# GpSimd folds three modulation vectors, scores run two heads ahead, and a query chunk moves in between the heads of two memory attentions

## What is computed

```
q = (h @ w_q).reshape(bsz, seq, MEM_HEADS, MEM_HEAD_DIM)
k, v = jnp.split(mem_n @ w_kv, 2, axis=-1)
s = jnp.einsum("bshd,bmhd->bhsm", q, k).astype(jnp.float32) * (MEM_HEAD_DIM ** -0.5)
p = jax.nn.softmax(s, axis=-1).astype(v.dtype)
o = jnp.einsum("bhsm,bmhd->bshd", p, v).reshape(bsz, seq, D_MODEL)
return o @ w_o
```

```
mod = jax.nn.silu(c) @ w_mod[l] + b_mod[l]
sh1, sc1, gt1, sh2, sc2, gt2 = jnp.split(mod[:, None, :], N_MOD, axis=-1)
```

## Time and profile before

| | |
|---|---|
| timed runs | 1748.21, 1750.21, 1751.40 us; median 1750.21 |
| span of the profiled execution | 1743.7 us; what lies around a span is seen only in the timed runs |
| busy share of the span | PE 88%, PEld 76%, DVE 50%, ACT 38%, POOL 9% |
| A, B, C: scores to output projection | 178 to 200, 506 to 550, 608 to 630 us |

### The profile page before, as it was taken

One profiled execution on the slowest core, in us unless ns is written; L12 is line 12 of the kernel. 1 busy time (PEld: TensorE's weight loads), 2 busy tenths in 40 slices (PEclk: granted clock), 3 DMA queues, 4 the chain that ended last, 5 costly groups with the idle time before them and its releaser, 6 DMA issues.

```text
span 1743.7 us, 35055 instructions
## 1 busy us (share of the span) xinstructions
PE 1536.5 (88%) x14790; PEld 1321.3 (76%) x14790; DVE 875.3 (50%) x1263; ACT 659.4 (38%) x869; POOL 149.6 (9%) x188
## 2 busy tenths in 40 slices
PE   9999999999999999999999999799998564656568
PEld 8999899988989989998899799698874232323234
DVE  5765466645665556664587688956641010101011
ACT  5445355435444435543566744525441000000001
POOL 5800000000000000000106011130010000000000
PEclk9999999999999999999999999999999678787879
DMA  7765566774744757664454343002899999999995
GB/s 251 242 218 176 188 168 193 225 258 149 262 143 155 249 181 205 192 194 165 134 161 155 97 152 117 26 27 76 314 391 410 431 432 431 430 429 430 431 431 250
DMA packets 238133, 417.16 MB, mean 239 GB/s; under 512 B 13698, under 2 KB 213929, under 8 KB 228009
## 3 DMA queue, kind: packets, MB, share of 16 engines
q1 hardware_dynamic: 237817, 414.59, 66.0%
q10 hardware_dynamic: 176, 0.53, 0.1%
HBM read 414.04 MB, written 1.05 MB: 238 GB/s over the span
## 4 chain that ended last, share of the span: by engine, by line
issue 47%; PE 42%; DVE 4%; POOL 4%; ACT 3%; DMA 1%; DVEq 0%; SPq 0%; POOLq 0%; ACTq 0%
PE bank L429 4%; PE bank L431 4%; PE bank L430 4%; PE bank L1919 2%; PE bank L445 2%; PE bank L447 2%; PE bank L446 2%; PE bank L1075 1%; PE bank L1077 1%; PE bank L457 1%; PE bank L761 1%; PE bank L1076 1%; PE bank L458 1%; PE bank L459 1%; DVE cy L1433 1%
## 5 line engine op out<-in xcount | busy, mean ns | idle before, releaser
L250 DVE TENSOR_TENSOR w_lo<-w_raw,w_hi 128x2048 fp32r<-128x2048 f32 (+2 forms) x178 | 400.3, 2252 | 249.9 <-ACT w_hi L243 246.3
L243 ACT ACTIVATE w_hi<-w_raw 128x2048 fp32r<-128x2048 f32 (+2 forms) x178 | 334.0, 1881 | 152.4 <-DMA w_raw<-in_ffn_w_down_dram 61.7
L429 PE MATMUL bank<-h_hi,w_hi 128*128 128x256 f32 x1168 | 325.3, 279 | 7.0 <-DVE h_lo L639 3.7
L430 PE MATMUL bank<-h_lo,w_hi 128*128 128x256 f32 x1168 | 324.4, 278 | 0.0
L431 PE MATMUL bank<-h_hi,w_lo 128*128 128x256 f32 x1168 | 324.4, 278 | 0.0
L429 PEld LDWEIGHTS bank<-h_hi,w_hi 128*128 128x128 f32 x1168 | 220.3, 189 | 8.4 <-issue 8.3
L2799 PE MATMUL bank<-w_exp_four,xeT 128*32 128x256 f32 x1600 | 133.3, 502 | 99.0 <-DMA w_exp_four<-in_w_up_dram 59.2
L430 PEld LDWEIGHTS bank<-h_lo,w_hi 128*128 128x128 f32 x1168 | 220.4, 189 | 0.0
L431 PEld LDWEIGHTS bank<-h_hi,w_lo 128*128 128x128 f32 x1168 | 220.3, 189 | 0.0
L2799 PEld LDWEIGHTS bank<-w_exp_four,xeT 128*32 128x32 f32 x1600 | 67.0, 142 | 164.4 <-issue 87.5
L2932 ACT ACTIVATE sg<-bank 128x256 f32<-128x256 f32 x16 | 6.1, 384 | 391.4 <-PE bank L2799 391.4
(11 more groups left out here) (537 smaller groups left out, 3130.9 us busy)
## 6 DMA issues: line engine op xcount, KB each, us to landing
w_exp_four<-in_w_up_dram SPq DMA_DIRECT2D x13, 4096.0 KB, 33.3
w_exp_four<-in_w_down_dram SPq DMA_DIRECT2D x13, 4096.0 KB, 33.6
w_exp_four<-in_w_gate_dram SPq DMA_DIRECT2D x12, 4096.0 KB, 33.3
w_raw<-in_ffn_w_gu_dram SPq DMA_DIRECT2D x88, 512.0 KB, 5.1
w_raw<-in_w_in_dram SPq DMA_DIRECT2D x54, 512.0 KB, 4.6
w_mod<-in_w_mod_dram SPq DMA_DIRECT2D x24, 1024.0 KB, 6.9
w_raw<-in_ffn_w_down_dram SPq DMA_DIRECT2D x44, 512.0 KB, 4.2
w_raw<-in_mem_w_kv_dram SPq DMA_DIRECT2D x32, 512.0 KB, 4.6
```

The source lines that it names most:

```text
L243: e.activation(whi[slot][:, 0:w], raw[slot][:, 0:w], ACT.Copy).then_inc(S["hi_ready"], 1)
L250: e.tensor_tensor(wlo[slot][:, 0:w], raw[slot][:, 0:w], whi[slot][:, 0:w].bitcast(F32), ALU.subtract).then_inc(S["lo_ready"], 1)
L429: e.matmul(dst, whi[slot][:, lo:hi_], bh[:, k, :], start=begin, stop=False)
L430: e.matmul(dst, whi[slot][:, lo:hi_], bl[:, k, :], start=False, stop=False)
```

## The change

Three things. The vectors 1, 0 and 4 are folded on GpSimd (`fold`): each side buffer is multiplied by its part of silu(c), the buffers are added up, and the two halves of the sum too, so that 1024 columns are left; four matmuls with a column of ones (`modulate_folded`) then sum over the partitions, at the last head. Those attentions run `by_parts`: scores and softmax of two heads ahead of the first turn, then scores of head h+2 behind the turn of head h. In the memory attentions the query gemm has three chunks, and the fourth is a `chunk_in_parts` whose halves lie behind the first scores and in head 0; the scores wait for their own query chunk alone. All other attentions go as before.

```diff
-        gemm(4, cols(A["mem_w_q"][l]), fm_chunk(*into), act_chunk=copy_fm(qT), ready=[tx], act_ready=[tx],
+        gemm(3, cols(A["mem_w_q"][l]), fm_chunk(*into), act_chunk=copy_fm(qT), ready=[tx], act_ready=[tx],
              beside={j: mod_load(4, 2 + j) for j in range(2)} if l else None)
+        fold(vector)
+        q_evacs = st.evac_a
+        keys_ready, values_ready = (S["act_evac"], q_evacs - 3), dve_evacs()
+        last_queries = chunk_in_parts(cols(A["mem_w_q"][l], first=768), [fm_part(*into, f) for f in range(2)],
...
-        to = attention(4, 2, 256 ** -0.5, score, vv, (pb0, pb1), ptb, [act_evacs(), dve_evacs()], free=[all_used()],
-                       vector=vector)
+        to = attention(4, 2, 256 ** -0.5, score, vv, (pb0, pb1), ptb,
+                       lambda h: [values_ready, (S["act_evac"], q_evacs - 2 + h)], free=[all_used()],
+                       vector=vector, parts=last_queries)
...
+    fold(0)
     k_first = keys2_part(0)
...
-                   causal=causal, free=[all_used()], vector=0, beside={h: lambda: next(memory_side) for h in range(8)})
+                   causal=causal, free=[all_used()], vector=0, parts=memory_side)
...
+        def by_parts():
+            tp = {h: softmax(h, scores(h)) for h in range(2)}
+            next(parts, None)
+            for h in range(heads):
+                tc = turn(h, tp[h])
+                if h + 2 < heads:
+                    tp[h + 2] = softmax(h + 2, scores(h + 2))
+                next(parts, None)
+                if h == heads - 1:
+                    modulate_folded(vector)
+                tl = values(h, tc)
+                tls.extend([tl] * kts)
+            return tl
...
+    def fold(v_):
+
+        n_ = MOD_ORDER.index(v_)
+        scaled = {}
+        for j in range(4):
+            scaled[j] = pool.do(lambda e, j=j: e.tensor_tensor(
+                side[j][:, :, :], side[j][:, :, :], csil[:, 2 * j:2 * j + 2].rearrange("p (k a) -> p k a", a=1).broadcast_to((P, 2, D)),
+                ALU.mult), (side_in[j], 16 * (n_ + 1)), t_cw)
+            if j % 2:
+                t = pool.do(lambda e, j=j: e.tensor_tensor(side[j - 1][:, :, :], side[j - 1][:, :, :], side[j][:, :, :], ALU.add),
+                            scaled[j - 1], scaled[j])
+                scaled[j - 1] = t
+        t = pool.do(lambda e: e.tensor_tensor(side[0][:, :, :], side[0][:, :, :], side[2][:, :, :], ALU.add), scaled[0], scaled[2])
+        t = pool.do(lambda e: e.tensor_tensor(side[0][:, 0, :], side[0][:, 0, :], side[0][:, 1, :], ALU.add), t)
+        folded[v_] = t
...
+            for c in range(4):
+                ins = e.matmul(G[3][32 * c:32 * c + 32, 0:MW], cw[:, :, :].rearrange("p k n -> p (k n)")[:, 64 - v_:96 - v_],
+                               side[0][:, 0, c * MW:(c + 1) * MW], start=True, stop=True)
+            ins.then_inc(mod_used, 4)
```

More of the change, by code:

```diff
@@ L684, in norm_to_features, with attention @@
         return split_features(turn_rows(xn, rows), gain, free)
-    def attention(heads, kts, scale, score, v, pbuf, ptbuf, ready, causal=None, free=(), vector=None, beside=None, behind=None, ahead=None):
+    def attention(heads, kts, scale, score, v, pbuf, ptbuf, ready, vector=None, causal=None, free=(), parts=None, beside=None, behind=None, ahead=None):
         t_soft, t_pt, t_pv = {}, {}, {}
@@ L696, in scores @@
             b = h % 2
-            w = list(ready) + ([xfree[b]] if xfree[b] else []) + ([t_soft[h - 2]] if h >= 2 else [])
+            w = list(ready(h) if callable(ready) else ready) + ([xfree[b]] if xfree[b] else []) + ([t_soft[h - 2]] if h >= 2 else [])
             tok = None
@@ L774, in attention, with by_heads @@
         tls = []
[L775 to L796, removed]
+        def by_parts():
[11 more added lines that the diff above has]
+            return tl
+        def by_heads():
+            ts = scores(0)
+            tp = softmax(0, ts)
+            for h in range(heads):
+                if h + 1 < heads:
+                    ts = scores(h + 1)
+                if h == 0 and "first" in beside:
+                    beside["first"]()
+                if h in ahead:
+                    ahead[h]()
+                tc = turn(h, tp)
+                if h + 1 < heads:
+                    tp = softmax(h + 1, ts)
+                if h in beside:
+                    beside[h]()
+                tl = values(h, tc)
+                tls.extend([tl] * kts)
+                if h in behind:
+                    behind[h]()
+            return tl
+        tl = by_parts() if parts else by_heads()
         tiles_of[tl] = tls
@@ L830, in build @@
     t_cw0 = pool.do(lambda e: e.memset(cw[:, :, :], 0.0))
+    t_cw0 = pool.do(lambda e: e.memset(cw[:, 1, 0:1], 1.0), t_cw0)
     t_z0 = pool.do(lambda e: e.memset(zT[:, :, 0:CONV1 - 1], 0.0))
@@ L861, in modulate, with modulated, modulate_folded, run_pe @@
         if j == 3:
[L862 to L869, removed]
+            modulated(n_)
+    def modulated(n_):
+        done = (mod_used, 4 * n_ + 4)
+        if n_ == 0:
+            t = dve.do(lambda e: e.tensor_copy(mrow[:, :], G[3][:, 0:MW]), done)
+        else:
+            t = dve.do(lambda e: e.tensor_tensor(mrow[:, :], mrow[:, :], G[3][:, 0:MW], ALU.add), done, t_mod["row"])
+        bank_free[3] = [t]
+        t_mod["row"] = t
+    t_mod, folded = {}, {}
+    def fold(v_):
[12 more added lines that the diff above has]
+        folded[v_] = t
+    def modulate_folded(v_):
+        n_ = MOD_ORDER.index(v_)
+        free = list(bank_free[3])
+        def run_pe(e):
+            for w in free:
+                e.wait_ge(*w)
+            e.wait_ge(*folded[v_])
+            for c in range(4):
+                ins = e.matmul(G[3][32 * c:32 * c + 32, 0:MW], cw[:, :, :].rearrange("p k n -> p (k n)")[:, 64 - v_:96 - v_],
+                               side[0][:, 0, c * MW:(c + 1) * MW], start=True, stop=True)
+            ins.then_inc(mod_used, 4)
+        pe.raw(run_pe)
+        modulated(n_)
     mem_in = nc.alloc_semaphore("mem_in")
@@ L989, in mem_attention @@
             gemm(1, cols(W, first=D + 768), tm_chunk(*features), act_chunk=copy_tm(vv, first=768), beside={0: mod_load(4, 1)})
-        gemm(4, cols(A["mem_w_q"][l]), fm_chunk(*into), act_chunk=copy_fm(qT), ready=[tx], act_ready=[tx],
+        gemm(3, cols(A["mem_w_q"][l]), fm_chunk(*into), act_chunk=copy_fm(qT), ready=[tx], act_ready=[tx],
              beside={j: mod_load(4, 2 + j) for j in range(2)} if l else None)
+        fold(vector)
+        q_evacs = st.evac_a
+        keys_ready, values_ready = (S["act_evac"], q_evacs - 3), dve_evacs()
+        last_queries = chunk_in_parts(cols(A["mem_w_q"][l], first=768), [fm_part(*into, f) for f in range(2)],
+                                      act_chunk=lambda e, c, u, ch: e.activation(
+                                          qT[:, 6:8, :], G[u][:, :].rearrange("p (k t) -> p k t", k=2), ACT.Copy))
         def score(e, h, t_, dst):
```

## The result

The changed kernel took 1763.15 us (median of 5 runs, 1758.62 to 1766.39), the kernel before 1750.66 (5 runs beside it). The ratio is 1.0063, 95% interval 1.0044 to 1.0082: 12.5 us slower. The forecast was 1767, range 1741 to 1775.

A forecast was written before the change was run, and what follows sets the result against it. TensorE was taken to bound the kernel. It gains 13.3 us, but waits from fold operations alternating with VectorE's splits leave A 5.8, B 2.0 and C 8.9 us slower, 16.7 on 1750.2: forecast 1767 us, range 1741 to 1775.

The forecast's parts named there:

- Sign and cause: Whole kernel: slower (chance 0.69), because GpSimd's fold and VectorE exclude each other; 13.3 us of TensorE gain outweighed, net 16.7.
- A: First memory attention: waits of 9.3 us less 3.5 us of gain, 5.8 us slower.
- B: MoBA attention: waits of 8.3 us less 6.3 us of gain, 2.0 us slower.
- C: Second memory attention: waits of 12.4 us, 7.2 of them for head 0's probabilities, less 3.5 of gain, 8.9 slower.
- B's 6.3 us of gain: MoBA attention without modulation quarters in its heads: 37.0 us instead of 43.3.
- Eight heads of 4.47 us: MoBA attention: every head takes 4.47 us, plus an uncovered last turn of about 1.2 us, 37.0 us together.
- GpSimd's operations: Fold on GpSimd: each operation over 128x2048 takes 4.6 us, a whole fold 34.6 us.
- B's lateness: MoBA attention: chunk splits late by 4.2 us in all, then 4.1 us of waiting for the rope, sum 8.3.
- Small operations I let pass: VectorE's small operations on statistics and a softmax's pair of scalings: counted as not held up by the fold.
- Alternation: While a fold runs: one GpSimd operation, one chunk split, 6.9 us per chunk where TensorE wants one in 5.65.
- Rivals 1 and 2: VectorE goes first when both wait: 1743.6 us, chance 0.15; wide operations do not exclude each other: 1737 us, chance 0.10.
- Rival 3, the clock: Granted clock also falls after each of the three long waits, some 1.7 us each: 1772 us, chance 0.11.

The follow-up runs named there:

- e1_no_fold: Changed kernel without the eight GpSimd operations of each fold, so its modulation vectors are not the reference's; ratio 0.9957 to the kernel before.
- e7_nofold_border: Changed kernel without the fold work, MoBA attention's softmax of head h+2 written behind the values of head h; ratio 0.9982 to the kernel before.
- e9_moba_old: Changed kernel with TensorE's quarters in the last two heads instead of the fold, and the MoBA attention as before; 1746.28 us, ratio 0.9969.
- e5: Changed kernel with each wide GpSimd operation of the fold cut into two over 128x1024; ratio 1.0043 to the kernel before.
- e10: Changed kernel with the memory attentions' scaled negative maximum and scaling of probabilities done on ScalarE instead of VectorE; 1767.00 us, ratio 1.0074.
- e11: As e10, and in A and C the fold starts only when VectorE has scaled the norm's rows; 1768.25 us, ratio 1.0082.
- e12: As e11, with the fold in pieces over 128x1024; 1761.86 us, ratio 1.0045.
- e6: Changed kernel with TensorE's quarters in the last two heads instead of the fold, MoBA attention's softmax behind the values; 1750.79 us, ratio 0.9980.

## Why the forecast was right, point by point

**Sign and cause: right, and shown.** Taking the fold's operations out moves the ratio from 1.0063 to 0.9957. The price of the fold, changed kernel less e1_no_fold by stages, is A 5.1, B 7.6, C 9.1, sum 21.7 us; the gain without it 3.4, 1.4, 3.9, sum 8.7. Forecast were 30.0 and 13.3. The net (13.0 against 16.7) is near because both terms were too large, on opposite sides: the cause was right, that the number came so near is luck.

**The term that failed: B's 6.3 us of gain.** "Eight heads of 4.47 us" took the length of one head that waited for nothing (530.75 to 535.22); a later head without a quarter had waited 1.13 us for pb even before, which I passed over. In the new order the chain over ScalarE and VectorE (scores, softmax, copy, a_hi, a_lo, a split) exceeds the head in four of eight. e1_no_fold shows 1.4 us of gain, e7_nofold_border that it is a chain and not one bank, e9_moba_old that the old order is as good.

**GpSimd's operations were sized too long.** A sum over 128x2048 took 6.49 us behind a split of 2.29, so 4.2 for itself, and 4.62 in B where no split was ahead of it; but a multiplication by the broadcast column 11.27/2 − 2.29 = 3.35, where I had 4.6 for both. Four of a fold's seven wide operations are such: 5 us less a fold. In A two chunks ahead of the query gemm were late by 0.21 and 0.95 us, which makes 1.2 at the first query chunk (0.8 forecast), the second was not late (1.3) and the third by 0.70 (1.3). The first softmax was late by 1.56 instead of 4.4; the scores of head 3 waited 0.99 (1.5). In C they did not wait, where 4.8 were forecast: TensorE had already lost 7.06 us ahead of them. Where that first wait was shorter they did wait, 3.74 us in e5, 2.60 in e10 and 4.54 in e11.

**B's lateness** was forecast as 4.2 for chunks and 4.1 for the rope. The chunks were not late. GpSimd's timeline shows it waiting for side buffers that I had taken as landed, so the fold was less dense there:

```profile
459.35 4.55 POOL L895 TENSOR_TENSOR w_mod<-w_mod,csil 128x2048 f32<-128x2048 f32 x1 [4.23 <-DMA w_mod<-in_w_mod_dram]
466.01 5.70 POOL L895 TENSOR_TENSOR w_mod<-w_mod,csil 128x2048 f32<-128x2048 f32 x1 [2.11 <-DMA w_mod<-in_w_mod_dram]
471.85 4.62 POOL L899 TENSOR_TENSOR w_mod<-w_mod,w_mod 128x2048 f32<-128x2048 f32 x1
```

The rope's wait came at 4.56. What else B lost lies in its heads (1 us more of waits than in e1_no_fold) and in 1.50 us at the turn of C. So B's 7.6 us for 8.3 forecast are partly luck too: half of the 8.3 was chunks.

**"Small operations I let pass": wrong.** VectorE and GpSimd at the first softmax of C:

```profile
615.02 0.68 DVE L720 TENSOR_REDUCE small<-bank 128x2 f32<-128x512 f32 x1
615.73 3.74 DVE L721 TENSOR_SCALAR small<-small 128x2 f32<-128x2 f32 x1
620.76 1.52 DVE L729 TENSOR_SCALAR pb<-pb,small 128x256 f32<-128x256 f32 x2
```

```profile
613.09 6.36 POOL L902 TENSOR_TENSOR w_mod<-w_mod,w_mod 128x2048 f32<-128x2048 f32 x1
619.52 2.34 POOL L903 TENSOR_TENSOR w_mod<-w_mod 128x1024 f32<-128x1024 f32 x1
```

The scaled maximum (L721) took 3.74 us and ended with the fold operation, at 619.5; and the row scaling (L609), which I had run before the fold, lost the race to it: 4.09 us for 0.75, in A and in C. The pair in the earlier trace rows on which I rested this was not held; why not, no run shows. The Trainium skill (SBUF — State Buffer, "Who interferes with whom") names TENSOR_SCALAR among the operations that can take the shared pair, and the reduction as one that never does; the traces agree: 3.74 us for L721, 0.68 for L720 with a fold operation running. I had used only its line on two SBUF inputs. In C (3.6 us there and 0.9 for the pair of L729) this was 4.5 of the 7.06 us, and the late split the other 2.6. My 7.2 had some 4.8 for the late split and, against my own rule, 2.4 for a softmax behind the sixth GpSimd operation (probabilities at 615.9, where 610.7 and 2.8 give 613.5). So the two numbers agree partly by luck.

**Alternation: right** (5.9 us for a split where 2.29 is its own). Rivals 1 and 2 are refuted by that row: three splits in a row each waited, and the GpSimd operations between them too. **Rival 3, the clock, was partly true.** It was given 0.11 and stood beside the forecast, not in it. After the 7 us wait in C:

```profile
620.00:624.00 4.00, 1.67 (x6) 1.58 (x7) 2.45 (x5) 1.41 (x7) 1.86 (x1) 0.50 0.00 0
624.00:628.00 4.00, 4.00 (x22) 3.50 (x22) 2.82 (x4) 2.42 (x4) 0.00 (x0) 0.76 0.00 0
```

TensorE works again from 622.33, at 0.50 and then 0.76: (1.67 × 0.50) + (4.00 × 0.24) = 1.8 us lost, the 1.7 that I had for such a wait. After the 4.6 us wait in B the clock was 0.59 over 510 to 514, 1.6 us, but the kernel before has its own 1.7 in that place, so nothing is added. After A's waits it stayed at 1.00. In other kernels with a fold it cost more: 3.2 us in A of e10, 4.9 in B of e12. The loads (four side buffers freed at once) cost nothing that a wait shows.

## What to carry to other kernels

Work for an idle GpSimd is paid by VectorE where the two hold each other up as here: list VectorE's operations by inputs and kind before you price it, the smallest ones of the softmax too, and count how many stand in one chain, since each can wait for a whole operation of the other. Cutting the other's work into pieces helps only where few catchable operations stand in the chain. A wait that gets shorter is only gained if no later one on the same path takes it back. And before counting on shorter heads, add up the chains of all engines through one head, not TensorE's column alone.

## What the runs showed of the chip that I had not expected

The same matmuls run at two paces at a full granted clock. From 240 to 300 us lies the same feed-forward loop with no wait in it; first the kernel before, then e9_moba_old:

```profile
240.00:260.00 20.00, 20.00 (x179) 20.00 (x178) 12.35 (x16) 11.24 (x10) 0.00 (x0) 1.00 0.66 184
```

```profile
240.00:260.00 20.00, 20.00 (x172) 20.00 (x171) 11.53 (x16) 10.70 (x10) 0.00 (x0) 1.00 0.65 181
```

179 matmuls in 20 us against 172, 4% (a chunk is 48 matmuls in all, 16 times three, and not the 48 times three of my text on the kernel before). In seven profiled executions (e6 to e12) the 187 to 188 us from A's end to the next transpose of normed rows became 192 to 193. Whether it goes by execution or by program the runs don't say: each kernel has one profile. The clock's dips fall in one execution at the rope and in another in the heads (B at a mean of 0.99, 0.98 or 0.96). Both are a part of the scatter of single executions, 1743.65 to 1760.55 us for 26 runs of the kernel before; how much of it they make up is not shown. Effects of a few us are to be read by stages, with the clock beside them.
